# The order of VectorE's work in an MLP stage: one addition, some low parts and one weight split moved

## The reference, cut to what matters

```python
D_MODEL, SEQ, D_FF = 1024, 512, 4096

def rmsnorm(x, g, eps=1e-6):
    return x * rsqrt(mean(x * x, axis=-1, keepdims=True) + eps) * g

def sq_relu_mlp(h, w1, w2):          # w1: 1024 x 4096, w2: 4096 x 1024
    u = relu(h @ w1)
    return (u * u) @ w2

# per layer l:
x = x + (recurrent_block or diff_attention)(...)
x = x + sq_relu_mlp(rmsnorm(x, mlp_norm[l]), mlp_w1[l], mlp_w2[l])
# ... at the end
return rmsnorm(x, final_norm)
```

## Time and profile before

| | |
|---|---|
| median of 3 runs | 1066.61 us (1066.57 to 1066.99) |
| profiled execution, its own time | 1068.11 us |
| its span | 1066.3 us |
| mean granted TensorE clock | 0.994 |
| PE busy | 1035.3 us (97%), 5920 instructions |
| PEld busy | 884.0 us (83%) |
| DVE busy | 814.2 us (76%) |
| ACT busy | 647.0 us (61%) |
| POOL busy | 106.2 us (10%) |
| q1 (loads of SP and ACT), share of the 16 DMA engines | 30.6% |
| q0 (accumulations of POOL), the same | 27.5% |

### The profile page before, as it was taken

One profiled execution on the slowest core, in us unless ns is written; L12 is line 12 of the kernel. 1 busy time (PEld: TensorE's weight loads), 2 busy tenths in 40 slices (PEclk: granted clock), 3 DMA queues, 4 the chain that ended last, 5 costly groups with the idle time before them and its releaser, 6 DMA issues.

```text
span 1066.3 us, 15296 instructions
## 1 busy us (share of the span) xinstructions
PE 1035.3 (97%) x5920; PEld 884.0 (83%) x5920; DVE 814.2 (76%) x1157; ACT 647.0 (61%) x940; POOL 106.2 (10%) x133
## 2 busy tenths in 40 slices
PE   8999999999999999999999999999999999999996
PEld 5777889879979979978877777778979979978975
DVE  7889876885896886898656666566797697698697
ACT  6699865645745645655436656566764664664665
POOL 1000021220101101100000000012011011011012
PEclk9999999999999999999999999999999999999998
DMA  7222289598598598562421111257689589679672
GB/s 262 81 79 96 80 210 247 119 239 219 116 253 220 113 257 216 114 171 72 126 60 60 60 60 40 61 189 158 187 183 233 176 173 230 190 161 241 190 155 102
DMA packets 47592, 165.29 MB, mean 155 GB/s; under 512 B 5408, under 2 KB 5536, under 8 KB 47392
## 3 DMA queue, kind: packets, MB, share of 16 engines
q1 hardware_dynamic: 31536, 109.59, 30.6%
q0 software_dynamic: 15552, 53.48, 27.5%
q10 hardware_dynamic: 432, 1.24, 0.3%
HBM read 159.05 MB, written 2.10 MB: 151 GB/s over the span
## 4 chain that ended last, share of the span: by engine, by line
PE 68%; DVE 14%; issue 7%; DMA 6%; ACT 4%; POOL 1%; SPq 0%; DVEq 0%; POOLq 0%; ACTq 0%
PE ps L1832 21%; PE ps L1965 19%; PE ps L2000 16%; DVE w_lo L1120 5%; PE ps L2063 4%; DMA q<-weights 3%; PE ps L2122 2%; DMA w_raw<-weights 2%; ACT w_hi L618 2%; DVE r L1460 2%; PE ps L2148 2%; PE ps L1891 1%; DVE value L1498 1%; PE ps L2137 1%; DVE a_lo L1487 1%
## 5 line engine op out<-in xcount | busy, mean ns | idle before, releaser
L1965 PE MATMUL ps<-x_hi,w_hi 128*128 128x256 f32 x896 | 254.9, 284 | 2.5 <-DVE w_lo L1120 1.8
L1965 PE MATMUL ps<-x_hi,w_lo 128*128 128x256 f32 x896 | 254.3, 284 | 0.0
L1965 PE MATMUL ps<-x_lo,w_hi 128*128 128x256 f32 x896 | 254.2, 284 | 0.0
L1120 DVE TENSOR_TENSOR w_lo<-w_raw,w_hi 128x1024 fp32r<-128x1024 f32 x134 | 163.7, 1222 | 81.5 <-ACT w_hi L618 81.1
L618 ACT ACTIVATE w_hi<-w_raw 128x1024 fp32r<-128x1024 f32 x134 | 141.4, 1055 | 136.5 <-DMA w_raw<-weights 88.7
L1120 DVE TENSOR_TENSOR w_lo<-q,w_hi 128x1024 fp32r<-128x1024 f32 x144 | 177.0, 1230 | 58.7 <-ACT w_hi L618 57.9
L618 ACT ACTIVATE w_hi<-q 128x1024 fp32r<-128x1024 f32 x144 | 151.6, 1053 | 107.8 <-PE ps L1965 45.4
L2000 PE MATMUL ps<-w_hi,a_hi 128*128 128x512 f32 x448 | 177.1, 395 | 14.3 <-DVE value L1498 12.4
L1965 PEld LDWEIGHTS ps<-x_hi,w_hi 128*128 128x128 f32 x896 | 172.7, 193 | 3.4 <-DVE w_lo L1120 2.0
L2000 PE MATMUL ps<-w_hi,a_lo 128*128 128x512 f32 x448 | 175.2, 391 | 0.0
L2000 PE MATMUL ps<-w_lo,a_hi 128*128 128x512 f32 x448 | 175.2, 391 | 0.0
(11 more groups left out here) (218 smaller groups left out, 1651.2 us busy)
## 6 DMA issues: line engine op xcount, KB each, us to landing
w_raw<-weights SPq DMA_DIRECT2D x134, 512.0 KB, 4.3
q<-weights POOLq DMA_DIRECT2D x96, 512.0 KB, 8.3
q<-weights SPq DMA_DIRECT2D x64, 512.0 KB, 4.7
x<-x_t SPq DMA_DIRECT2D x8, 256.0 KB, 6.0
y_t<-value SPq DMA_DIRECT2D x8, 256.0 KB, 2.3
acc<-work POOLq DMA_DIRECT2D x6, 256.0 KB, 3.3
rstd<-work POOLq DMA_DIRECT2D x6, 256.0 KB, 5.1
w_raw<-weights SPq DMA_DIRECT2D x4, 256.0 KB, 4.8
```

Of the source, the lines that this page charges most:

```text
L1120: nc.vector.tensor_tensor(w_lo[:, t % RING, :], src, w_hi[:, t % RING, :], ALU.subtract).then_inc(wlo_done, 1)
L1965: ins = nc.tensor.matmul(to, w[:, t % RING, ws], o[:, op, j, :], start=fresh and j == 0 and f % 2 == 0 and n == 0, stop=j == PAIRS - 1 and ...
```

## The change

On VectorE, the order of `mlp` is written out as a list in place of a loop with conditions. In the down stage these places change:

- addition 1 goes from step 18 to directly behind addition 0, ahead of split 19
- addition 2 goes from ahead of split 23 to ahead of split 22
- low part 4 goes from ahead of split 21 to behind split 22

All other instructions of the stage keep their order: addition 3 is still directly ahead of split 25, addition 4 ahead of split 27, addition 5 ahead of the split of the next group's tile 1.

On ScalarE, high part 4 goes from step 17 to step 19 (behind w_hi of tile 22), high part 5 from step 19 to step 20 (behind tile 23).

At the start of a layer, the splits of tile 3 (w_hi and w_lo) come earlier: w_hi ahead of the last `sums_hi`, w_lo between the last two `lo_of`, ahead of both quarter sums; before, w_lo of tile 3 was made between the quarter sums.

```diff
@@ ScalarE, residual_step
                     if m == NCH - 1:
+                        split_hi(t + m + RING)
                         sums_hi(j)
-                        split_hi(t + m + RING)
                     square(layer, m)
@@ ScalarE, mlp
-                    for i, at in enumerate((9, 13, 14, 15, 17, 19, 21)):
+                    for i, at in enumerate((9, 13, 14, 15, 19, 20, 21)):
                         if s == at:
                             act_hi(layer, g, i)
@@ VectorE, residual_step
                 lo_of(PAIRS - 1, H21)
+                split_lo(t + NCH - 1 + RING)
                 lo_of(PAIRS - 1, T1)
@@ VectorE, mlp
-                for s in range(PER):
-                    i = s // 2 - NPROD - 1
...
-                    if s >= 16 and s % 2 == 0:
-                        add_product(layer, g, i)
-                    if s == 18:
-                        act_lo(layer, g, 4)
-                    if s < PER - 2 or not last:
-                        split_lo(up_tile(layer, g, s + RING - 1))
...
-                    elif s == 16:
-                        act_lo(layer, g, 3)
-                    elif s == 17:
-                        act_sum(layer, g, 4)
-                    elif s == 20:
-                        act_lo(layer, g, 5)
-                    elif s == 22:
-                        act_lo(layer, g, 6)
...
+                def split(s):
+                    if s < PER - 2 or not last:
+                        split_lo(up_tile(layer, g, s + RING - 1))
+
+                quarter_sum(layer, g, 0, 0)
+                if g:
+                    split(0)
+                quarter_sum(layer, g, 0, 1)
+                if g:
+                    add_product(layer, g - 1, NPROD - 1)
...
+                act_sum(layer, g, 3)
+                split(15)
+                if (layer, g) == (1, 0):
+                    dve.wait_ge(turned_read, 2 * QB)
+                if g == 0:
+                    dve.wait_ge(scale_done, layer + 1)
+                add_product(layer, g, 0)
+                add_product(layer, g, 1)
+                split(16)
+                act_lo(layer, g, 3)
+                split(17)
+                act_sum(layer, g, 4)
+                split(18)
+                add_product(layer, g, 2)
+                split(19)
+                act_lo(layer, g, 4)
+                split(20)
+                act_lo(layer, g, 5)
+                split(21)
+                add_product(layer, g, 3)
+                split(22)
+                act_lo(layer, g, 6)
+                split(23)
+                add_product(layer, g, 4)
...
```

More of the change, by code:

```diff
@@ L1546, in mlp @@
+                if g:
+                    add_product(layer, g - 1, NPROD - 1)
+                for s in range(1, 8):
+                    split(s)
                     if (g, s) == (0, 4):
                         norm_newton((N_M0, N_M1)[layer])
-                    if s == 10:
-                        act_lo(layer, g, 0)
-                    elif s == 13:
-                        act_lo(layer, g, 1)
-                        act_sum(layer, g, 2)
-                    elif s == 14:
-                        act_lo(layer, g, 2)
-                    elif s == 16:
-                        act_lo(layer, g, 3)
-                    elif s == 17:
-                        act_sum(layer, g, 4)
-                    elif s == 20:
-                        act_lo(layer, g, 5)
-                    elif s == 22:
-                        act_lo(layer, g, 6)
@@ L1563, in mlp @@
-                    if after is not None and s == PER - 1:
-                        after(NPROD - 2)
+                up_sum(layer, g, 0)
+                split(8)
+                split(9)
+                up_sum(layer, g, 1)
+                split(10)
+                act_lo(layer, g, 0)
+                split(11)
+                quarter_sum(layer, g, 1, 0)
+                up_sum(layer, g, 2)
+                split(12)
+                quarter_sum(layer, g, 1, 1)
+                act_sum(layer, g, 1)
@@ new lines, in mlp @@
+                split(13)
+                act_lo(layer, g, 1)
+                act_sum(layer, g, 2)
+                split(14)
+                act_lo(layer, g, 2)
+                act_sum(layer, g, 3)
[7 more added lines that the diff above has]
+                split(16)
@@ L1565, in mlp @@
+                split(24)
+                split(25)
+                add_product(layer, g, 5)
+                split(26)
+                split(27)
                 if last:
+                    after(NPROD - 2)
                     add_product(layer, g, NPROD - 1)
```

18 lines of the change are left out of this document (removed).

## The result

The changed kernel takes 1058.95 us (median of 4 runs, 1057.29 to 1059.15); the kernel before took 1066.8 us beside it (4 runs, 1066.57 to 1067.96). The ratio is 0.992, interval 0.9904 to 0.9936: 0.8% faster, clear of the scatter, but 9.5 us above the forecast of 1049.4 and outside its range. One of e11's four executions ran at a mean clock of 0.751, took 1269.14 us and is left out of its numbers here.

The account below looks back on a forecast made before the run. TensorE, busy 97%, was taken as the bound, so only its idle time could be won: 13.7 + 0.4 + 1.7 + 1.0 + 0.4 = 17.2 us off the median 1066.61 gives 1049.4 us, range 1046.4 to 1055.

Parts of the forecast that it names:

- The group part: Eight down stages: 13.7 us from TensorE's gaps before tile 20, 0.4 from small bubbles there, 1.7 from the clock.
- The margin at tile 24: Down stage: addition 3 ready 0.5 us before tile 24 in the second group, -0.4 in the fourth; 0.6 us subtracted overall.
- That edit costs nothing: ScalarE, down stage: high part 4 moved behind w_hi of tiles 21 and 22 fills idle time, still starting at 297.1.
- The clock of the first group: First group's down stage: the half-speed stretch at 217.6 to 221.0 goes with the gap ahead, returning 1.7 us.
- Rival B: Low clock stays or falls elsewhere, such as at small new waits: 1051.1 to 1053 us, chance 0.10.
- The start edit: Layers' starts: moving tile 3's splits earlier shortens TensorE's waits, 1.0 us in the second layer and 0.4 in the first.
- 0.8 us is free at once: Second layer, before tile 6: this much won immediately, up to 0.7 us more if the load lands as much sooner.
- SP and POOL issue in the order of before: Down stage: issue order stays, only tile 25's load goes out some 2.4 us sooner and tile 19's w_lo comes 0 to 0.2 later.
- The new wait for squares at 739: Second layer's start: sums of squares reach their semaphore 5.1 us after POOL's issue, giving a new wait near 737 to 739.
- A: Down stage: tile 25's load takes bandwidth from tile 24's, costing 1 us in each group: 1057.4 us, chance 0.14.
- C: Down stage: the moved addition 1 ends late and delays split 19; at 2.5 us a group, near 1070 us, chance 0.02.
- D: Down stage: the gap reappears whole at tile 22 or 24 because VectorE is the bound: 1066 us, chance 0.04.

Follow-up runs that it names:

- e11: The changed kernel run again without any edit, on another chip: 1056.84 us, ratio 0.9882 to the kernel before.
- e7: e4 with POOL's multiplications of result rows at the end held until the last weight split is done: 1055.87 us, ratio 0.9862.
- e8: e4 with high parts 4 and 5 on ScalarE back in steps 17 and 19, VectorE's order as changed: 1067.84 us, ratio 0.9985.
- e5: e4 with the norm's first step, and in layer 2 ScalarE's second pair of turned rows, ahead of tile 7's splits: 1054.14 us, ratio 0.9851.
- e12: e3 with low part 4 ahead of split 21 again, ScalarE's order as changed: 1061.14 us, ratio 0.9928.
- e3: The changed kernel with the first quarter sum moved ahead of the split of tile 3: 1053.89 us, ratio 0.9860.
- e4: The changed kernel with POOL's two accumulations in each layer's first group held until both quarter sums are done: 1051.83 us, ratio 0.9843.
- e2: The kernel before with only the edit at the layers' starts (splits of tile 3 earlier): 1071.78 us, ratio 1.0027.
- e1: The changed kernel with its edit at the layers' starts undone, the down stage as changed: 1053.94 us, ratio 0.9865.
- e9: e3 with the norm's first step and turned rows ahead of tile 7's splits, and POOL's row multiplications behind the last split: 1054.10 us, ratio 0.9851.
- e10: e9 without the edit on POOL's row multiplications: 1052.01 us, ratio 0.9839.

## Why the prediction was wrong

The span came out 8.0 us above the forecast: 7.1 at the starts of the layers (1.4 won by the forecast, 5.7 lost), 0.6 in the down stages, 0.5 ahead of the first group, less 0.2 behind the last tile. The other 1.5 us of the 9.5 are the step from span to median: the prediction took over from the kernel before that the median lies 1.5 us below the profiled execution, and here it lies at it (1058.95 and 1058.89).

- **The group part, 13.7 + 0.4 + 1.7 us: right.** 15.8 us were forecast for the eight down stages, 15.2 measured. The wait on the additions is gone, split 19 was not moved (0.1 a group was subtracted for it), and a group takes 78.77 us for the 78.8 foreseen. The margin at tile 24 fell as feared: in the groups of layer 2 the steps of tiles 23 and 24 show 0.2 to 0.4 us too much, about 1.0 in all by the steps where 0.6 was subtracted. The last group won only 0.66: there its last tiles waited 1.2 us for the long split that e7 looks at, for which the prediction had no term. The kernel before had a split of 2.32 us there as well, but slack for it.
- **"That edit costs nothing", of the high parts on ScalarE: right as to cost, but short.** e8 shows that the gain hangs on it: without it the time is 13.7 us above e5, nearly all that the down stages had won. The prediction had looked at what covers the moved instruction, not at what stands behind it if it isn't moved. For low part 4 the same holds for about half of the gain (e12: 7.3 us).
- **The clock of the first group, 1.7 us: right for its place, taken back elsewhere.** The stretch at 217.6 is high now. In the profiled execution as low a stretch stands at layer 1's start. The other execution of the changed kernel (e11) has none at layer 1 and one of twice the length at layer 2: in both the low stretches ahead of the last down stage's end add up to 6.8 us, as in the kernel before, so in sum nothing of this term was kept. With the loads put right, e3 and e4 had no such stretch at all. Rival B had named such small waits; its range of 1051.1 to 1053 counts one or two stretches in all, not the 1.7 on top, as its words have it.
- **The start edit, +1.4 us: wrong, and this is the step that failed.** -5.7 us were measured in the profiled execution, against ends of 0.2 to 2.2. Of these, 1.5 are the low clock in layer 1, which e11 does not show there, and about 1.2 are layer 2's late tile 1, which is scatter. By the medians the edit costs 2.9 us in e2, and 5.9 or 1.8 by e1 against the two runs of the changed kernel: the size is uncertain, the sign is not, as e2's interval and every landing agree. The prediction put it as "0.8 us is free at once and up to 0.7 more if the load lands as much sooner". Both halves are false. The load was issued sooner and landed later: tile 7's in layer 1 went out at 8.07 relative, not 8.88, and landed at 18.79, not 17.33; in layer 2, with the 1.2 us of its late tile 1 taken off, at 12.3, not 13.1, and landed at 22.8, not 22.2. A landing is not the issue plus a fixed time: it had been 4.7 us for tile 6 when the load went out 0.1 us behind the first of POOL's accumulations and ahead of the second, and it is 7.0 behind both (3.7 and 3.6 where e3 and e4 take them away). The Trainium skill, "DMA: Bandwidth & Descriptors", section "Issuing engines are not separate DMA queues", which the prediction used for the loads of tile 25, says that DMAs of all issuers run on the same 16 engines and interleave. The trace agrees: SP's load and POOL's accumulations are issued by two engines, and still the load's time hangs on which goes out first. And the 0.8 us were not free: the turned rows of layer 2 stood behind the same load on ScalarE, and TensorE needed them ahead of tile 6. The rows for this were there: 748.39 on VectorE and 749.38 on TensorE leave 1 us, and TensorE turned x in it, from 748.59 on.
- **The omission that made it so:** of the moved w_hi I counted what it did to VectorE's order and to SP's load, not to POOL. It lets ScalarE's squares end 0.7 us earlier relative to tile 0, and POOL's list hangs on them. "SP and POOL issue in the order of before" was said of the down stage and held there; at the start it was never asked.
- **The wait of 1.80 us for w_lo of tile 3 went, as forecast** (the step of tile 2 to 3 in layer 2: 4.91 before, 2.95 after). The new wait for squares at 739 did not come; their DMA landed 3.4 us after its issue, not 5.1. In e1, e3, e9, e10 and e12 it did come, with 0.3 to 1.2 us. Layer 2's tile 1 waited 1.3 us for x_lo, which no edit here touches; that step was 3.9 to 5.2 us over all the kernels, so about 1 us of layer 2's loss is scatter.
- **The rivals.** A was the right mechanism in the wrong place: loads and accumulations in each other's way, not at tile 24 but at the starts. That its 1057.4 is near the 1058.95 measured is luck: it was the price of 1 us in each of eight down stages. C did not occur: addition 1 ended at 292.70 and split 19 began at 292.73. D did not.

The forecast's 1049.4 is 0.984 of the kernel before. e4 (0.9843) and e10 (0.9839), with the loads put right, come near that. It does not bear out the forecast's terms: e4's up stages of the first groups won 2.9 us where 1.4 were foreseen, and its down stages 15.1 for the 15.8.

Open: why e5 to e8 wait at addition 0 of the first group; and what makes the clock fall. It fell behind or within waits of 2.0 to 3.4 us at the layers' starts, yet not in e11's layer 1 behind the same wait of 2.0; it stayed high behind all eight waits of 1.5 to 1.9 us for the additions in e2 and fell behind one of eight in the kernel before (1.85 us). In layer 2 it also fell in tile 3 or 4 of e1, e5 to e8, e9 and e10, where TensorE makes the norm's statistics and turns x, behind waits of 0.2 to 0.9 us (in e1 one of 1.8 us stood 5.8 us earlier).

## What to carry to other kernels

An instruction moved ahead on one engine makes everything between its old place and its new one start earlier or later, and with it the DMA issues of other queues that wait for it: list each queue that hangs on it, and compare the order of the issues across queues before and after, not the times within one. Where a transfer is on the path, a hold on the accumulations ahead of it, or an earlier start of the load itself, can be worth more than the time won on an engine (here the load took 7.0 us behind the accumulations and 3.6 or 3.7 ahead of them). And where a wait is taken off one engine's list, look at what the other engines do at the head of theirs: without the moves on ScalarE nearly all of this gain was gone (e8), and without the later low part on VectorE half of it (e12).

## What the runs showed of the hardware

- A load of 512 KB from SP took 3.6 to 5.1 us when it was issued ahead of POOL's two accumulating DMAs or within 0.2 us of the first (both layers of the kernel before, e1, e3 to e10 and e12), and 6.8 to 7.1 us when it was issued 1.4 us behind the first and so behind both (both layers of the changed kernel, e2 and e11).
- A VectorE subtraction of 128x1024 fp32 with both inputs in SBUF took 2.32 us beside a multiplication of POOL, 1.22 alone. The subtraction ahead of it, beside POOL's first multiplication, took 1.22, and POOL's took 2.40 where it takes 1.28 to 1.29 in e7: one of the two engines paid, not always the same. The Trainium skill, "SBUF — State Buffer", section "Who interferes with whom", says that a VectorE instruction with two SBUF inputs contends with a GpSimd one that reads SBUF, for ports that only one of them can hold. The trace agrees, and e7, which parts the two in time, shows the short durations alone.
- The granted clock behind the same wait before tile 6 of layer 1 was 0.50 in one execution of the changed kernel (2.05 us) and 1.00 in another (2.00 us).
